# Two-layer decoder on one core: the last FFN block's gate and up columns loaded and multiplied as one panel of two full halves

## What is computed

```python
for l in range(2):
    x = layer_norm(ALPHA * x + hybrid_mixer(x, ...), ...)
    x = layer_norm(ALPHA * x + memory_cross_attention(x, mem, ...), ...)
    if l == 0:                                   # dense SwiGLU, F_DENSE = 2816
        gate, up = split(x @ w13, 2)             # w13: 1024 x 5632
        f = (silu(gate) * up) @ w2               # w2: 2816 x 1024
    else:                                        # 8 experts, two per token, F_MOE = 3584
        f = moe_swiglu(x, router, w13, w2)
    x = layer_norm(ALPHA * x + f, ...)
```

## Time and profile before

| | |
|---|---|
| median of 3 runs | 1818.96 us (1817.24 to 1819.96) |
| the profiled execution | 1814.82 us, its span 1813.0 us |
| PE busy | 1722.1 us, 95% of the span |
| PEld busy | 1378.6 us, 76% |
| DVE busy | 1331.1 us, 73% |
| ACT busy | 1017.5 us, 56% |
| DMA | 465.98 MB, mean 257 GB/s |
| granted TensorE clock, mean | 0.979 |

### The profile page before, as it was taken

The page is one execution under the profiler, slowest core; times in us unless marked ns, Lnnn a source line. Parts: engine busy times, 40 slices in busy tenths (PEclk is TensorE's granted clock), DMA queues, the critical chain, the costliest instruction groups (busy, mean ns, idle before and its releaser), DMA issues.

```text
span 1813.0 us, 21662 instructions
## 1 busy us (share of the span) xinstructions
PE 1722.1 (95%) x7978; PEld 1378.6 (76%) x7978; DVE 1331.1 (73%) x1229; ACT 1017.5 (56%) x895; POOL 22.2 (1%) x32
## 2 busy tenths in 40 slices
PE   7989979999999999789999999999999999999996
PEld 5845767888777468677888888888888888888884
DVE  4465745545454666459989889899898898998996
ACT  4344333434333442337777777677777776777772
POOL 0001000000000010000000000000000000000000
PEclk9999989999999999979999999999999999999998
DMA  8512433645634234179999999999999999999991
GB/s 293 177 57 92 162 117 103 222 151 197 210 138 141 93 117 139 47 275 350 366 337 369 359 355 364 339 365 371 343 363 369 339 368 357 352 367 341 364 370 42
DMA packets 206471, 465.98 MB, mean 257 GB/s; under 512 B 11952, under 2 KB 14544, under 8 KB 206416
## 3 DMA queue, kind: packets, MB, share of 16 engines
q1 hardware_dynamic: 200880, 463.76, 71.6%
q10 hardware_dynamic: 5536, 1.48, 0.3%
HBM read 464.16 MB, written 1.05 MB: 257 GB/s over the span
## 4 chain that ended last, share of the span: by engine, by line
PE 88%; DVE 6%; ACT 2%; issue 1%; DMA 1%; DVEq 0%; ACTq 0%; SPq 0%
PE ps L1542 21%; PE ps L1993 16%; PE ps L1995 16%; PE ps L1994 16%; PE ps L1571 4%; PE ps L1911 3%; PE ps L1970 2%; PE ps L1979 1%; DVE w_lo L959 1%; PE ps L1837 1%; PE ps L1507 1%; PE ps L1697 1%; PE ps L1819 1%; PE ps L1752 1%; DVE ring_r L947 1%
## 5 line engine op out<-in xcount | busy, mean ns | idle before, releaser
L959 DVE TENSOR_TENSOR w_lo<-ring,w_hi 128x2048 fp32r<-128x2048 f32 x336 | 768.0, 2290 | 112.4 <-ACT w_hi L630 109.4
L630 ACT CAST w_hi<-ring 128x2048 fp32r<-128x2048 f32 x336 | 642.2, 1912 | 278.3 <-PE ps L1995 263.1
L1993 PE MATMUL ps<-w_hi,xe_hi 128*128 128x512 f32 x896 | 353.1, 394 | 1.8 <-DVE w_lo L959 1.8
L1995 PE MATMUL ps<-w_hi,xe_lo 128*128 128x512 f32 x896 | 349.3, 390 | 0.0
L1994 PE MATMUL ps<-w_lo,xe_hi 128*128 128x512 f32 x896 | 348.7, 389 | 0.0
L1542 PE MATMUL ps<-ring_r,xT_r 128*128 128x512 f32 (+1 forms) x704 | 188.2, 397 | 10.2 <-DVE late_r L938 10.2
L1993 PEld LDWEIGHTS ps<-w_hi,xe_hi 128*128 128x128 f32 x896 | 168.2, 188 | 37.1 <-DVE w_lo L959 2.8
L1995 PEld LDWEIGHTS ps<-w_hi,xe_lo 128*128 128x128 f32 x896 | 168.2, 188 | 35.7
L1994 PEld LDWEIGHTS ps<-w_lo,xe_hi 128*128 128x128 f32 x896 | 168.4, 188 | 33.7
L1993 PE MATMUL ps<-w_hi,he_hi 128*128 128x512 f32 x448 | 178.1, 397 | 0.0
L1995 PE MATMUL ps<-w_hi,he_lo 128*128 128x512 f32 x448 | 174.8, 390 | 0.0
(11 more groups left out here) (266 smaller groups left out, 1759.3 us busy)
## 6 DMA issues: line engine op xcount, KB each, us to landing
ring<-in_moe_w_dram SPq DMA_DIRECT2D x336, 1024.0 KB, 5.3
ring<-in_ffd_w_dram SPq DMA_DIRECT2D x31, 1024.0 KB, 5.2
ring<-in_w_in_dram SPq DMA_DIRECT2D x24, 1024.0 KB, 5.4
ring<-in_xa_wkv_dram SPq DMA_DIRECT2D x16, 1024.0 KB, 5.0
ring<-in_w_out_dram SPq DMA_DIRECT2D x8, 1024.0 KB, 5.0
ring<-in_xa_wq_dram SPq DMA_DIRECT2D x8, 1024.0 KB, 5.3
ring<-in_xa_wo_dram SPq DMA_DIRECT2D x8, 1024.0 KB, 5.2
ring<-in_ffd_w_dram SPq DMA_DIRECT2D x4, 512.0 KB, 3.5
```

Of the source, the lines that this page charges most:

```text
L630: act.copy(w_hi[:, q % SPLIT_SLOTS, :], ring[:, q % RAW_SLOTS, :]).then_inc(hi_ready, 1)
L959: dve.tensor_tensor(w_lo[:, q % SPLIT_SLOTS, :], ring[:, q % RAW_SLOTS, :], w_hi[:, q % SPLIT_SLOTS, :].bitcast(F32), ALU.subtract).then_i ...
L1993: pe.matmul(ps[:, bank, :], x_hi, hi[:, c, cols], start=first, stop=False)
L1995: return pe.matmul(ps[:, bank, :], x_lo, hi[:, c, cols], start=False, stop=last)
```

## The change

The gate's last 256 columns and the up's last 256 columns become one panel of 512, `TAIL`, of two full halves: in each row of a half, 256 gate columns and then 256 up columns. Panel `TAIL + 1` leaves the list, which then has 97 halves where it had 99. SP loads such a half with two transfers of 512 KB (`landed` counts them both). TensorE runs four half-length `gemm`s: gate over the first half, up over the first half, gate over the second, up over the second, so that four banks are open at once. In ScalarE's and VectorE's block loops the last pair of splits is left out for block 5. The core of the diff:

```diff
+TAIL = MIX_PANELS + 2 * FFN_CHUNKS - 2
+TAIL_COLS = F_DENSE - (FFN_CHUNKS - 1) * N
-DENSE_HALVES = [(l, n, g) for l in range(DEPTH) for n in range(L1 if l == 0 else MIX_PANELS)
+DENSE_HALVES = [(l, n, g) for l in range(DEPTH) for n in range(L1 if l == 0 else MIX_PANELS) if n != TAIL + 1
                 for g in range(1 if n == L1 - 1 else 2)]
...
             if n < 2 * FFN_CHUNKS:
-                width = min(N, F_DENSE - n // 2 * N)
-                return cols(a["ffd_w13"][0], (n % 2) * F_DENSE + n // 2 * N, width)
+                both = a["ffd_w13"][0].rearrange("(c p) (h n) -> p c h n", p=P, h=2)
+                return both[:, :, :, F_DENSE - TAIL_COLS:]
...
+        def landed(at):
+            return 16 * sum(2 if DENSE_HALVES[i][1] == TAIL else 1 for i in range(at % DENSE_SLOTS, at + 1, DENSE_SLOTS))
...
             else:
-                u = acc_use(l, n)
+                u = acc_use(l, TAIL + 1 if n == TAIL else n)
                 engine.wait_ge(acc_ready[2 * (u % 2) + 1], u // 2 + 1)
...
-                    sp.dma_start(raw_half(l, n, g), dense_src(l, n, g)).then_inc(dense_in[at % DENSE_SLOTS], 16)
+                    into, src = raw_half(l, n, g), dense_src(l, n, g)
+                    if n == TAIL:
+                        for h in range(2):
+                            sp.dma_start(into[:, :, h * TAIL_COLS:(h + 1) * TAIL_COLS], src[:, :, h, :])
...
 # ScalarE, end of a block
-                        if n < FFN_CHUNKS:
+                        if n < FFN_CHUNKS - 1:
                             split_high(2)
...
 # VectorE, end of a block
-                        if n < FFN_CHUNKS:
+                        if n < FFN_CHUNKS - 1:
                             split_low(2)
...
 # gemm
-                _, _, w = w_panel(l, n).shape
+                own, c0, w = (n - n % 2, n % 2 * TAIL_COLS, TAIL_COLS) if TAIL <= n <= TAIL + 1 else (n, 0, N)
...
-                        if t == 0:
+                        if t == 0 and n == own:
                             half_ready(l, n, g)
...
-                        if t == T - 1 and g == 0:
+                        if t == T - 1 and g == 0 and n != TAIL:
                             ins.then_inc(dense_used, 1)
...
+                        elif n == FFN_CHUNKS - 1:
+                            gemm(l, TAIL, chunks=range(KC // 2))
+                            gemm(l, TAIL + 1, chunks=range(KC // 2))
+                            gemm(l, TAIL, chunks=range(KC // 2, KC))
+                            gemm(l, TAIL + 1, chunks=range(KC // 2, KC))
```

More of the change, by code:

```diff
@@ L375, in w_panel @@
                 n -= count
+            if n < 2 * FFN_CHUNKS - 2:
+                return cols(a["ffd_w13"][0], (n % 2) * F_DENSE + n // 2 * N)
             if n < 2 * FFN_CHUNKS:
-                width = min(N, F_DENSE - n // 2 * N)
-                return cols(a["ffd_w13"][0], (n % 2) * F_DENSE + n // 2 * N, width)
+                both = a["ffd_w13"][0].rearrange("(c p) (h n) -> p c h n", p=P, h=2)
+                return both[:, :, :, F_DENSE - TAIL_COLS:]
             n -= 2 * FFN_CHUNKS
@@ L389, in dense_view @@
         def dense_view(buffer, l, n, g):
-            _, c, w = dense_src(l, n, g).shape
+            c = dense_src(l, n, g).shape[1]
+            w = D if n >= L1 - W2_P else N
             return buffer[:, 0:c * w].rearrange("p (c n) -> p c n", c=c)
@@ L475, in dense @@
                         wait_used(sp, at - DENSE_SLOTS)
-                    sp.dma_start(raw_half(l, n, g), dense_src(l, n, g)).then_inc(dense_in[at % DENSE_SLOTS], 16)
+                    into, src = raw_half(l, n, g), dense_src(l, n, g)
+                    if n == TAIL:
+                        for h in range(2):
+                            sp.dma_start(into[:, :, h * TAIL_COLS:(h + 1) * TAIL_COLS], src[:, :, h, :])                                .then_inc(dense_in[at % DENSE_SLOTS], 16)
+                    else:
+                        sp.dma_start(into, src).then_inc(dense_in[at % DENSE_SLOTS], 16)
             for l in range(DEPTH):
                 for n in range(L1 if l == 0 else MIX_PANELS):
-                    dense(l, n)
+                    if n != TAIL + 1:
+                        dense(l, n)
                     if l == 0 and n == 1:
@@ L607, in split_high @@
                     at = HALF_AT[name]
-                    act.wait_ge(dense_in[at % DENSE_SLOTS], 16 * (at // DENSE_SLOTS + 1))
+                    act.wait_ge(dense_in[at % DENSE_SLOTS], landed(at))
                     if HIGH_BEFORE[name]:
@@ L1522, in half_ready @@
                     at = HALF_AT[l, n, g]
-                    pe.wait_ge(dense_in[at % DENSE_SLOTS], 16 * (at // DENSE_SLOTS + 1))
+                    pe.wait_ge(dense_in[at % DENSE_SLOTS], landed(at))
             def gemm(l, n, tiles=range(T), chunks=range(KC)):
                 u = acc_use(l, n)
-                _, _, w = w_panel(l, n).shape
+                own, c0, w = (n - n % 2, n % 2 * TAIL_COLS, TAIL_COLS) if TAIL <= n <= TAIL + 1 else (n, 0, N)
                 for t in tiles:
@@ L1540, in gemm @@
                             for c in range(4):
-                                weights = low_half(l, n, g)[:, c, :] if q else high_chunk(l, n, g, c)
-                                ins = pe.matmul(ps[:, b, 0:w], acts[p][:, 4 * g + c, t * P:(t + 1) * P], weights,
+                                weights = low_half(l, own, g)[:, c, :] if q else high_chunk(l, own, g, c)
+                                ins = pe.matmul(ps[:, b, 0:w], acts[p][:, 4 * g + c, t * P:(t + 1) * P],
+                                                weights[:, c0:c0 + w],
                                                 start=(g == 0 and m == 0 and c == 0), stop=(g == 1 and m == 2 and c == 3))
-                        if t == T - 1 and g == 0:
+                        if t == T - 1 and g == 0 and n != TAIL:
                             ins.then_inc(dense_used, 1)
```

## The result

The changed kernel takes 1827.03 us (median of 5 runs, 1825.75 to 1827.63) against 1818.96 us (5 runs, 1814.58 to 1820.44): ratio 1.0047, 95% interval 1.0033 to 1.006. The medians differ by 8.1 us; the forecast was 8.4, and the interval allows 6.0 to 10.9. Its profiled execution took 1825.75 us, with a span of 1823.9 us where the kernel before had 1813.0: 10.9 us more. TensorE's busy time hardly grew (1725.4 us, 95% of the span; VectorE 1331.1, ScalarE 1016.4), the traffic is the same 465.98 MB, and the chain still lies on TensorE for 89%.

A forecast was written before the change was run, and what follows sets the result against it. The chain lay on TensorE for 88% of the span, so only TensorE's waits counted. Terms of 2.1 + 6.3 = 8.4 us on the median of 1818.96 gave 1827.4 us (+0.46%), range 1822.0 to 1830.8.

The forecast's parts named there:

- The split order: End of FFN block 5: w3's split, waiting for its home, holds VectorE's products, so w2 starts later: +2.1 us.
- the first rival: Only the slot counts: w3's home free early or products not behind it, so no split-order term: 1825.3 us, chance 0.10.
- The slow stretch: First 12 matmuls of w2 at reduced clock: already paid after the shorter wait, so 0 added, 0.3 to 0.5 us at most.
- The slot: Before the first expert: half 0 waits for (15, 0), so its load and ScalarE's first expert split come later: +6.3 us.
- What was said to cost nothing: In the FFN: four open banks cost nothing, two-part loads are covered, fewer splits save less than half a microsecond per engine.
- the earlier w2: Faster rival: early splits bring w2 forward, 4.3 us in all; with the slot's turn hidden too, 1814.7 us, chance 0.05.
- Slower at 0.85: Whole kernel: chance 0.85 of a slower result, beyond the 0.2% bound at 1822.6 us; the forecast itself had 0.62.
- Slower still: Rival: both terms, plus a longer wait before the first expert keeping the gather and expert matmuls at 1.2 GHz: 1830.5, chance 0.13.

The follow-up runs named there:

- Products first: Changed kernel with no pair of splits ahead of block 5's products, both pairs behind them, on both engines: ratio 1.0017 to the kernel before, median 1820.44 us.
- four splits ahead: Kernel before with all four splits of block 5 (w0 to w3) ahead of its products on both engines, none behind: ratio 1.0044, 8.0 us.
- The slot alone: Kernel before with dense half i in ring slot (i + 3) % 5, so expert half 0 takes over half (15, 0); FFN untouched: ratio 1.0037, 6.7 us.
- its removal: Changed kernel with dense half i in ring slot (i + 2) % 5, so expert halves take over the same dense halves as before: ratio 1.0017.
- with both terms out: Changed kernel with no splits ahead of block 5's products and ring slot (i + 2) % 5: ratio 0.998, 1812.03 against 1816.53 us.
- one split ahead: Kernel before, no merged panel, with only w0 split ahead of block 5's products and w1 to w3 behind, on both engines: ratio 0.9985.
- `low(0)` behind the norm: Changed kernel with VectorE's split of expert half 0 moved behind the residual and norm of tile 1: ratio 1.0029 to the kernel before.

## Why the prediction came out right, point by point

**The split order, +2.1.** Measured +2.3. The steps held singly: w3's high part went to `late_r`, its split started at the end of block 5 (427.34, with the 0.7 taken off 426.6, for 426.4), its load wasn't late, the products followed VectorE's 2.29. Products first takes the term away; four splits ahead in the kernel before makes a wait of the same kind, by a late load. One condition was given wrongly: the first rival said that the term is 0 if w3's home were free early. By the rows above it would be 0.13 us less and no more. The prediction's own figures said so, with VectorE's split of w2 ending at 428.25 and that of w3 starting at 428.35, but it named the home alone as the cause.

**The slow stretch, 0 to 0.5.** Measured 0.8, the term most mis-sized. I had said that the stretch after 2.55 us of waiting was paid already. Mostly so, but the granted clock of the stretch went from 0.63 to 0.51, and the 12 matmuls took 5.39, 5.37 and 5.33 us in the three traces that have this wait:

```profile
432.90:438.30 5.40, 5.31 (x13) 4.15 (x14) 1.11 (x2) 0.00 (x0) 0.00 (x0) 0.51 0.02 5
774.40:780.00 5.60, 5.60 (x24) 4.54 (x25) 2.73 (x4) 0.00 (x0) 0.54 (x1) 1.00 0.00 0
```

(windows of the changed kernel: us, busy PE, PEld, DVE, ACT, POOL, then the granted clock). The Trainium skill's page "TensorE: Matmul & The Clock Gate", section "HAM oscillation — how this bites in real kernels", has a cold start follow a wait that is long enough. The 4.87 us agree with it, but the shorter wait wasn't free, and behind 10.62 us in the kernel with four splits ahead the clock was 0.67 and the 12 matmuls took 4.36 us, so the length of the wait alone doesn't give the price here.

**The slot, +6.3.** Measured +6.3: the first expert split at 789.05 less 778.46 less the 4.3 us that all was later. The value was right to 0.1 because it wasn't an estimate: in the kernel before another load waited for the very same half. The slot alone costs 6.7 us in the kernel before, its removal gives 5.4.

**What was said to cost nothing.** Four open banks, the two-part loads, the halved number of small splits: with both terms out the kernel isn't slower than the old one with w2 as early, which speaks against a cost of more than about 2 us. The two-part load landed in 4.5 us for each part and nothing waited for it. The new matmul order isn't free of effect, though: it makes the gate's sum and its `Silu` late, and by the rows above this alone costs nearly the whole first term once two splits stand between them and the products. What I had put only as a rival, the earlier w2, is real: it needs both of its conditions, nothing late ahead of the products and the slot, and its 4.3 us then show as 3.6, within the interval. But it is the order's and not the merged panel's, as one split ahead in the kernel before gives it too.

**What wasn't foreseen.** The first 12 matmuls of panel 14, partly at half clock before (4.57 us, granted clock 0.62 from 768.5 to 773), ran at full clock in the changed kernel (5.80 us for 24; the second window above), which gave 1.6 us back. But 24 matmuls about 22 us earlier took 8.61 us where they took 7.10 before, so this came to nothing. The kernel with `low(0)` behind the norm does the same work as the changed one up to here and has 7.11 and 7.34 us. Such shifts are those of single executions.

**Luck in the number.** The terms that the trace bears out, 2.3, 0.8 and 6.3, make 9.4 us, and the profiled pair lies 10.9 apart; the medians lie 8.1 apart, inside the interval of 6.0 to 10.9. The mechanism was right, but that the forecast of 8.4 is only 0.3 off is partly luck: it left out the 0.8 us, and the interval reaches 2.5 us to either side.

**The chances.** Slower at 0.85 was borne out. The rival of the slot's term alone, 1825.3, lies under the lowest run by only 0.45; it is refuted by products first and not by the time. Slower still, 1830.5, lies above the highest run, and its mechanism isn't there: the 32 gather matmuls take 5.94 us for 5.90 before, at a granted clock of 0.64 both times.

## What to carry to other kernels

When a list of buffers gets shorter or longer, follow each index that is taken from it modulo something, to the end of the program: the costliest part of this change was a ring slot in another layer's last panel, whose new owner was wanted first. When work is put into fewer pieces, count again which piece each fixed position in another engine's order now names, and what that one waits for; a split that can only come late in a block, be it for its buffer or for what stands ahead of it in its engine's order, must not stand ahead of what frees the block's banks. For the price of a load that will be asked for later, look for one that waits for the same event today, and read when it lands.

## What the runs showed of the hardware

- Stretches of TensorE at half clock differ between executions of the same work. The changed kernel and the one with `low(0)` behind the norm are alike up to panel 15. Yet 24 matmuls near 752 us took 8.61 us in one and 7.11 in the other, and the 24 of panel 14, behind a wait of 2.1 us both times, 5.80 and 7.34:

```profile
752.90 8.61 PE ps L1557 x24
```

```profile
771.23 7.34 PE ps L1557 x24
```

(the changed kernel, whose panel 14 stands above, then the one with `low(0)` behind the norm). So a difference of 1 or 2 us between two traces, in a place that the edit doesn't touch, is not to be put down to the edit.
- After the wait before w2, 12 matmuls took 4.58 us behind 2.55 us of idling and 5.39 behind 4.87, but 4.36 behind 10.6 (the kernel before with four splits ahead), and 3.02 behind none: the price doesn't simply grow with the wait.
- A load of 1024 KB landed after 4.8 to 5.2 us in most of the chains here (4.79, 5.08, 5.12, 5.18, 5.19, 5.22), after 6.27 and 6.30 (from `w_in`) at the start of layer 1, and after 7.21 us in the kernel with four splits ahead, which was 2.1 us of end time where it stood in the chain.
